# The third mixer of a two-layer hybrid block: one score product for both directions, one modulation job behind each step, fewer splits at stage borders, and transposes moved one stage ahead

## The chip, the core and the metric
One core of a Trainium2 chip runs one program. TensorE (PE) multiplies, VectorE (DVE) and ScalarE (ACT) work on elements, GpSimd (POOL) does little here, and SyncE (SP) issues the DMA transfers. Each has its own queue of instructions, run in order, and they are tied together by semaphores. The metric is device time in microseconds (us), the median of several runs.

## The reference
A diffusion backbone of two layers over 256 context and 256 latent tokens (512 columns in all, `T`) of width 1024. Each layer has a token-mixing part of four parallel mixers of 256 columns (RWKV-7, differential attention, HGRN2, mLSTM), read from one input projection and joined by one output projection, and a gated MLP with a centred convolution. Shift, scale and gate of each sub-layer come from a conditioning vector (`_adaln`: a matrix-vector product with `ada_w`). The third mixer, HGRN2, is a gated linear attention, run forward and on reversed time, and the two outputs are added:
```python
diff = b[:, :, :, None, :] - b[:, :, None, :, :]
pair_decay = jnp.where(causal[:, :, None], jnp.exp(jnp.minimum(diff, 0.0)), 0.0)
att = jnp.einsum('bhtd,bhsd,bhtsd->bhts', qc, kc, pair_decay)
o = jnp.einsum('bhtd,bhdv->bhtv', qc * jnp.exp(b), S) + jnp.einsum('bhts,bhsv->bhtv', att, vc)
```
Here `b` is the running sum of log forget gates, so the decay between two tokens is the exponential of a difference, per channel. The two directions have the same queries and values, and keys and gates of their own. Layer 1 needs outputs for the latent tokens only.

## The kernel before, in words
Tokens lie along the free axis, channels on the 128 partitions; 512 tokens are 4 blocks of 128. Activations are kept in SBUF from beginning to end and weights are streamed. All large products are made in three passes of a high and a low part (`product`, L235 to L237); the two parts of a weight tile are made by ACT (`split_high`, L224) and DVE (`split_low`, L228).

A layer is a row of stages, each a block of five instruction queues that ends when all five are done: `front` (modulation, first tiles of the input projection), `diff_attention`, `mlstm`, `hgrn`, `rwkv`, then the output projection and MLP. The input projection (`Projection`) runs through the first three: its tiles are shared out over the steps of those mixers. Tile t+2 is split while tile t is copied out of PSUM (`leave_act`, `leave_dve`; `act_turn`, `dve_turn` per step), so at each border the stage that ends has split one tile more than its successor needs to begin (`end + 1`).

In `hgrn` (L1510 on) the decays inside a block of 128 are factored by levels. At level l (0 to 6) the block is cut into pairs of halves of 2^l tokens; tokens of the one half attend to tokens of the other with respect to the value of `b` at the border, so that query and key factors are exponentials that stay at most 1. There are 7 levels and 2 directions d, so 14 steps `steps`, walked by all engines:
- DVE subtracts the border value (`exponents`, L1788); ACT takes exponentials for keys and queries (`exps`, L1922, L1925); DVE multiplies by queries (L1796) and keys (L1797) (`factors`);
- PE makes the scores into PSUM (L1669), 32 matmuls for two pairs of blocks in layer 0, 16 for one pair in layer 1;
- DVE takes the entries of that level out with a masked copy (`collect`, L1815) into `at`, 2 x 2048 columns, one matrix per direction, which POOL has zeroed (L1760).

Beside the steps run key decays (a subtraction on DVE, L1850, and an exponential of 1024 columns on ACT, L1955), keys, queries, transposes (L1652), products and states for what passes between blocks. The read-out multiplies `at` of both directions by the values (L1711).

Behind the scores also stand the **jobs**: the modulation products of parts of `ada_w` for what comes later. A job is four transfers of 512 KB into four slots (SP, L1612), each freed by the matmuls of the job before (PE, `job_blocks`, L446), a copy of the sums by ACT (`row_out`, L1934), a spread over the partitions by PE (L1637 for coefficients, L1639 for gates, once for each side, context and latent), and an addition by DVE (L465 or L1779). `HIDDEN` lists 10 jobs for layer 0 and 4 for layer 1, and `places(n)` shares them over the steps. The tail of `hgrn` prepares the low-rank parts and the keys of `rwkv` (table load L1972, scans L1447) and the norm. `rwkv` begins with 32 transposes on PE (L2093: V, be, ks, al), which ACT and DVE (L2456) copy out.

## Time and profile before
| what | value |
|---|---|
| median of 3 runs | 1746.48 us (1746.31 to 1747.27) |
| profiled execution | 1743.03 us |
| its span | 1740.9 us |
| mean granted TensorE clock | 0.956 |
| PE busy | 1595.0 us, 92% |
| DVE busy | 1089.4 us, 63% |
| ACT busy | 636.7 us, 37% |
| POOL busy | 75.5 us, 4% |

The span is the time between the first and the last instruction that the profile shows. Busy shares are a mean over stages that differ: most of PE's time lies in the projections and the MLP.

### The profile page before, as it was taken

Reading aid. Unit: us, or ns where it says so; the run is one execution under the profiler, and the core shown is the slowest. Engines: PE = TensorE matmul, PEld = TensorE weight load, DVE = VectorE, ACT = ScalarE, POOL = GpSimd, SP = SyncE. Lnnn points to the kernel's source line nnn. Section 1 sums busy time; section 2 is a strip of 40 time slices with the busy share of each in tenths; the row PEclk is TensorE's granted clock in tenths of the full one; section 3 lists DMA queues with packets and bytes.
Section 4 is the critical chain, followed back from the end, with each engine's and each line's share of the span. In section 5 each row is a group of like instructions: output and inputs, shape, how many; then the busy total and the mean of one; then the engine's idle time right before and its main releaser. Section 6 shows DMA issues by size and latency. Waiting matters only on the chain. (4 is left out here: it accounts for less than half of the span.)

```text
span 1740.9 us, 29515 instructions
## 1 busy us (share of the span) xinstructions
PE 1595.0 (92%) x12140; PEld 1267.4 (73%) x12140; DVE 1089.4 (63%) x1870; ACT 636.7 (37%) x1060; POOL 75.5 (4%) x112
## 2 busy tenths in 40 slices
PE   6999999878889999999999979999977799899997
PEld 4766776655678778888888867677764587678885
DVE  2287347887786674554453364745678867578776
ACT  4255222333531245222222252433243431366662
POOL 0000011200101000000000000000020100000000
PEclk8999999978999999999999989999978899999998
DMA  9411111077301034222223022112225101255551
GB/s 391 149 49 50 49 61 52 22 250 247 136 3 51 26 146 154 104 96 92 102 84 119 1 87 86 61 49 85 74 86 178 68 3 51 77 212 197 186 203 47
DMA packets 41622, 182.02 MB, mean 105 GB/s; under 512 B 4753, under 2 KB 5521, under 8 KB 33681
## 3 DMA queue, kind: packets, MB, share of 16 engines
q1 hardware_dynamic: 41488, 180.14, 29.0%
q8 instruction: 96, 1.57, 0.4%
q14 instruction: 38, 0.30, 0.1%
HBM read 179.08 MB, written 1.05 MB: 103 GB/s over the span
## 5 line engine op out<-in xcount | busy, mean ns | idle before, releaser
L235 PE MATMUL ps<-hr_in,wr_in 128*128 128x512 f32 (+1 forms) x544 | 221.8, 408 | 14.4 <-DVE wr_in L228 13.9
L236 PE MATMUL ps<-hr_in,wr_in 128*128 128x512 f32 (+1 forms) x544 | 209.1, 384 | 0.0
L237 PE MATMUL ps<-hr_in,wr_in 128*128 128x512 f32 (+1 forms) x544 | 208.5, 383 | 0.0
L235 PEld LDWEIGHTS ps<-hr_in,wr_in 128*128 128x128 f32 x544 | 108.4, 199 | 63.9 <-issue 35.4
L228 DVE TENSOR_TENSOR wr_in<-mix,wr_in 128x1024 fp32r<-128x1024 f32 x68 | 83.8, 1234 | 93.5 <-ACT wr_in L224 89.6
L235 PE MATMUL ps<-mix_r,work_r 128*128 128x512 f32 (+1 forms) x352 | 133.8, 380 | 1.6 <-DVE work_r L228 1.6
L236 PE MATMUL ps<-work_r 128*128 128x512 f32 (+1 forms) x356 | 135.1, 379 | 0.0
L228 DVE TENSOR_TENSOR work_r<-pr,work_r 128x2048 fp32r<-128x2048 f32 x38 | 86.9, 2288 | 67.7 <-ACT work_r L224 63.6
L237 PE MATMUL ps<-mix_r,work_r 128*128 128x512 f32 x320 | 124.5, 389 | 0.0
L237 PEld LDWEIGHTS ps<-hr_in,wr_in 128*128 128x128 f32 x544 | 108.3, 199 | 19.6
L236 PEld LDWEIGHTS ps<-hr_in,wr_in 128*128 128x128 f32 x544 | 108.8, 200 | 15.5 <-issue 0.2
L2988 PE MATMUL ps<-mix_r,work_r 128*128 128x512 f32 x336 | 116.7, 391 | 1.0 <-DVE mix_r L228 1.0
L224 ACT CAST wr_in<-mix 128x1024 fp32r<-128x1024 f32 x68 | 71.3, 1050 | 106.6 <-PE ps L237 102.5
L224 ACT CAST work_r<-pr 128x2048 fp32r<-128x2048 f32 x40 | 76.1, 1902 | 65.9 <-PE ps L237 65.9
L3293 ACT ACTIVATE pr<-work 128x512 f32<-128x512 f32 (+1 forms) x44 | 23.1, 525 | 192.9 <-DVE work L3161 192.9
L235 PE MATMUL ps<-work_r,mix_r 128*128 128x512 f32 x232 | 90.4, 390 | 1.0 <-DVE work_r L228 1.0
L236 PE MATMUL ps<-work_r,mix_r 128*128 128x512 f32 x232 | 90.3, 389 | 0.0
L2989 PE MATMUL ps<-mix_r,work_r 128*128 128x256 f32 x320 | 89.6, 280 | 0.0
L235 PEld LDWEIGHTS ps<-mix_r,work_r 128*128 128x128 f32 x352 | 66.2, 188 | 14.5 <-DVE work_r L228 2.0
L236 PEld LDWEIGHTS ps<-work_r 128*128 128x128 f32 x356 | 66.9, 188 | 12.5
L228 DVE TENSOR_TENSOR work_r<-ring,work_r 128x2048 fp32r<-128x2048 f32 x24 | 54.9, 2288 | 32.9 <-ACT work_r L224 30.4
L2988 PEld LDWEIGHTS ps<-mix_r,work_r 128*128 128x128 f32 x336 | 62.8, 187 | 15.5 <-issue 1.8
(525 smaller groups left out, 3312.1 us busy)
## 6 DMA issues: line engine op xcount, KB each, us to landing
mix<-in_w_in SPq DMA_DIRECT2D x68, 512.0 KB, 3.7
pr<-in_w_up SPq DMA_DIRECT2D x28, 1024.0 KB, 4.9
pr<-in_ada_w SPq DMA_DIRECT2D x40, 512.0 KB, 6.3
ring<-in_w_up SPq DMA_DIRECT2D x16, 1024.0 KB, 4.8
ring<-in_ada_w SPq DMA_DIRECT2D x28, 512.0 KB, 4.5
pr<-in_w_down SPq DMA_DIRECT2D x14, 1024.0 KB, 5.0
pr<-in_ada_w SPq DMA_DIRECT2D x8, 1024.0 KB, 15.6
work<-in_w_out SPq DMA_DIRECT2D x16, 512.0 KB, 4.1
```

What stands on the lines that cost most here:

```text
L224: return nc.scalar.copy(high, raw)
L228: return nc.vector.tensor_tensor(low, raw, high.bitcast(F32), ALU.subtract)
L235: nc.tensor.matmul(out, sh, mh, start=first, stop=False)
L236: nc.tensor.matmul(out, sh, ml, start=False, stop=False)
L237: return nc.tensor.matmul(out, sl, mh, start=False, stop=last)
L2988: nc.tensor.matmul(up_bank(f, v)[:, :], sh, hr[0][:, k * T:(k + 1) * T], start=k == 0, stop=False)
L2989: mm = nc.tensor.matmul(up_bank(f, v)[:, SIDE:], sl, hr[0][:, k * T + SIDE:(k + 1) * T], start=False, stop=k == KD - 1)
L3293: nc.scalar.activation(pr[:, f * T + lo0:(f + 1) * T], tb[:, (f % 2) * T + lo0:(f % 2 + 1) * T], ACT.Gelu_apprx_tanh).then_inc(S("gelu"), 1)
```

## The change
It has four parts.
- **Third mixer.** The steps are eight: the diagonal (`None`: raw queries times the sum of both directions' keys, taken out by a product with the identity, which also writes the zeros) and the seven levels in the order 0 to 4, 6, 5. A level's keys of both directions lie in one tile (the halves that are sooner in time for forward, later for backward) and so do its queries, and one score product serves both. `at` is one matrix of 2048 columns, so the read-out has half the matmuls. The last level (6, step `WHOLE`) is copied by ACT, 8 plain copies, rather than collected by DVE. The key decays are 16 exponentials of 128 columns on ACT with a bias each, without DVE's subtraction. The masks in the constants serve both directions.
- **Jobs.** One job stands directly behind each step's scores in layer 0 (8 jobs) and behind six of the eight in layer 1; jobs (1,2) and (1,3) replace (1,6) and (1,7) in the late list, which go into layer 1's third mixer. The gate's bias is loaded once and not for each side.
- **Borders.** The stage that ends no longer splits tile `end + 1`; the next stage does it at its beginning.
- **Transposes.** Those of V and ks (16) move from the beginning of `rwkv` to the end of `hgrn` on PE.

PE in the loop of layer 0, from the values' transposes on: scores of a step (L1669, then L1679), job matmuls (L446, then L447), coefficient spread (L1637, L1643), gate spread (L1639, L1645). Before:

```order
L1652 MATMUL ps<-const,pr 128x128 x8
L1669 MATMUL ps<-ring,work 128x128 x32
L446 MATMUL ps<-ring,cond 32x256 x8
L446 MATMUL ps<-pr,cond 32x256 x8
L1669 MATMUL ps<-ring,work 128x128 x16
L1637 MATMUL ps<-const,rowb 128x2 x4
L446 MATMUL ps<-ring,cond 32x256 x8
L446 MATMUL ps<-pr,cond 32x256 x8
L1669 MATMUL ps<-ring,work 128x128 x16
L1652 MATMUL ps<-const,pr 128x128 x8
```

and now:

```order
L1658 MATMUL ps<-const,pr 128x128 x8
L1679 MATMUL ps<-pr,work 128x128 x16
L447 MATMUL ps<-ring,cond 32x256 x8
L447 MATMUL ps<-pr,cond 32x256 x8
L1679 MATMUL ps<-ring,work 128x128 x16
L1643 MATMUL ps<-const,rowb 128x2 x4
L447 MATMUL ps<-ring,cond 32x256 x8
L447 MATMUL ps<-pr,cond 32x256 x8
L1645 MATMUL ps<-rowb,const 128x512
L1679 MATMUL ps<-ring,work 128x128 x16
L1645 MATMUL ps<-rowb,const 128x512
```

A job now stands behind each group of scores from the first on, and a level's two groups are one, made of the shared tiles.

DVE at the same place, from the first exponents (L1788, then L1797 and L1799). Before, up to the second collect:

```order
L1788 TENSOR_TENSOR work<-hx 128x1024 x2
L1796 TENSOR_TENSOR ring<-work,pr 128x1024
L1797 TENSOR_TENSOR work<-work,pr 128x1024
L1788 TENSOR_TENSOR work<-hx 128x1024
L1850 TENSOR_TENSOR pr<-hx 128x1024
L1796 TENSOR_TENSOR ring<-work,pr 128x1024
L1797 TENSOR_TENSOR work<-work,pr 128x1024
L1788 TENSOR_TENSOR work<-hx 128x1024
L1815 COPY_PREDICATED work<-const,ps 128x4x128 x4
L1850 TENSOR_TENSOR pr<-hx 128x1024
L1796 TENSOR_TENSOR ring<-work,pr 128x256x2
L1797 TENSOR_TENSOR work<-work,pr 128x256x2
```

and now, with the key sum (L1806), level 0's key copies (L1810), the factors (L1814, L1815), the diagonal (L1832) and masked collects (L1834):

```order
L1806 TENSOR_TENSOR work<-pr 128x1024
L1797 TENSOR_TENSOR work<-hx 128x512 x2
L1799 TENSOR_TENSOR work<-hx 128x1024 x2
L1810 COPY work<-pr 128x512 x2
L1815 TENSOR_TENSOR ring<-ring,pr 128x1024
L1799 TENSOR_TENSOR work<-hx 128x1024 x2
L1832 TENSOR_TENSOR work<-ps,const 128x4x128 x4
L1814 TENSOR_TENSOR work<-work,pr 128x256x2 x2
L1815 TENSOR_TENSOR ring<-ring,pr 128x1024
L1799 TENSOR_TENSOR work<-hx 128x1024 x2
L466 SCALAR_TENSOR_TENSOR modc<-ps,modb 128x8
L1834 COPY_PREDICATED work<-const,ps 128x4x128 x4
```

The key decays' subtraction (L1850) is gone, and two subtractions of 1024 columns now stand for one level where before each stood in a step of its own.

PE at the end of `hgrn` and the start of `rwkv` (L2093, then L1768 and L2128), before:

```order
L446 MATMUL ps<-pr,cond 32x256 x8
L946 MATMUL ps<-work,const 128x512
L446 MATMUL ps<-pr,cond 32x256 x8
L1568 UNCONDITIONAL_BRANCH
L2113 UNCONDITIONAL_BRANCH
L2093 MATMUL ps<-const,pr 128x128 x8
L2093 MATMUL ps<-const,ring 128x128 x24
L2137 MATMUL ps<-ring 128x128 x48
```

and now:

```order
L447 MATMUL ps<-pr,cond 32x256 x8
L1768 MATMUL ps<-const,pr 128x128 x8
L1768 MATMUL ps<-const,ring 128x128 x8
L1570 UNCONDITIONAL_BRANCH
L2148 UNCONDITIONAL_BRANCH
L2128 MATMUL ps<-const,ring 128x128 x16
L2170 MATMUL ps<-ring 128x128 x48
```

Of the 32 transposes 16 stand ahead of the stage's end (the branch) and 16 behind it.

The core of the diff:

```diff
-LAST = (((1, 6), (1, 7)), ((1, 8), (1, 9)))
-HIDDEN = (((0, 8), (0, 4), (0, 9), (0, 5), (1, 0), (0, 10), (1, 1), (0, 11), (1, 2), (1, 3)),
-          ((1, 4), (1, 5), (1, 10), (1, 11)))
+LAST = (((1, 2), (1, 3)), ((1, 8), (1, 9)))
+HIDDEN = (((0, 8), (0, 4), (0, 9), (0, 5), (1, 0), (0, 10), (1, 1), (0, 11)),
+          ((1, 6), (1, 7), (1, 4), (1, 5), (1, 10), (1, 11)))
+HIDDEN_AT = (range(8), (0, 1, 2, 4, 5, 6))
...
         for t in self.started(i):
             if t > self.first:
                 self.leave_act(act, t - 1)
-                self.high(act, t + 1)
+            self.high(act, t + 1)
...
             for t in range(proj.end):
-                proj.low(dve, t + 2)
+                if t + 2 <= proj.end:
+                    proj.low(dve, t + 2)
...
-            proj.high(act, proj.end + 1)
...
-    steps = [(d, l) for l in range(LEVELS) for d in range(2)]
+    steps = (None, *range(LEVELS - 2), LEVELS - 1, LEVELS - 2)
+    WHOLE = 6
...
+    def parts_at(n):
+
+        if n not in HIDDEN_AT[layer]:
+            return (), ()
+        q = HIDDEN_AT[layer].index(n)
+        return range(begins[q - 1] + 1 if q else 0, begins[q]), range(begins[q], begins[q] + 1)
+
+    late = range(begins[-1] + 1, PLACES)
...
+            for n in range(len(steps)):
+                ahead, behind = parts_at(n)
+                for p in ahead:
+                    job(p)
                 pe.wait_ge(S("kf"), n + 1)
+                moving = queries[n % 2] if n else tiles(pr, T_HQ, 2)
...
+                            mm = nc.tensor.matmul(score_bank(n, m, q)[:, b * P:(b + 1) * P], keys[n % 2][q * HD:(q + 1) * HD, t0:t0 + P],
+                                                  moving[q * HD:(q + 1) * HD, t0:t0 + P], start=True, stop=True)
...
+                for p in behind:
+                    job(p)
...
-        @block.gpsimd
-        def _(pool):
-            nc.gpsimd.memset(at[:, :], 0.0).then_inc(S("at0"), 1)
+            pe.wait_ge(S("kk_max"), 1)
+            pe.wait_ge(S("lora_out"), 8)
+            for src, bank in ((tiles(pr, T_V, 2), 0), (R.ks, 2)):
+                for j in range(TILES):
+                    for i in range(2):
+                        nc.tensor.transpose(ps[bank + j // 2][:, (j % 2) * 256 + i * P:(j % 2) * 256 + (i + 1) * P],
+                                            src[:, i * T + j * P:i * T + (j + 1) * P], ident)
...
             def exponents(n):
 
-                d, l = steps[n]
-                cv, dv = blocks(tiles(cum, 2 * d, 2), l), blocks(expo[d], l)
-                ref = (1 << l) - 1 if d == 0 else 1 << l
-                if n >= 2:
-                    dve.wait_ge(S("kf"), n - 1)
-                nc.vector.tensor_tensor(dv, cv, cv[:, :, :, ref:ref + 1].to_broadcast(list(cv.shape)),
-                                        ALU.subtract).then_inc(S("dv"), 1)
+                l = steps[n]
+                for d in range(2):
+                    cv, dv = blocks(tiles(cum, 2 * d, 2), l), blocks(tiles(expo[n % 2], 2 * d, 2), l)
+                    ref = (1 << l) - 1 if d == 0 else 1 << l
+                    if l == 0:
+                        ins = nc.vector.tensor_tensor(dv[:, :, :, 1 - d:2 - d], cv[:, :, :, 1 - d:2 - d], cv[:, :, :, d:d + 1], ALU.subtract)
+                    else:
+                        ins = nc.vector.tensor_tensor(dv, cv, cv[:, :, :, ref:ref + 1].to_broadcast(list(cv.shape)), ALU.subtract)
+                ins.then_inc(S("dv"), 1)
...
             def factors(n):
-                d, l = steps[n]
-                dve.wait_ge(S("exps"), n + 1)
-                if n >= 2:
-                    dve.wait_ge(S("s_mm"), len(pairs) * (n - 1))
-                nc.vector.tensor_tensor(later(queries[d], d, l), later(expo[d], d, l), later(tiles(pr, T_HQ, 2), d, l), ALU.mult)
-                nc.vector.tensor_tensor(sooner(keys[d], d, l), sooner(keys[d], d, l), sooner(tiles(pr, T_HF + 2 * d, 2), d, l),
-                                        ALU.mult).then_inc(S("kf"), 1)
+
+                l, k = steps[n], keys[n % 2]
+                if n == 0:
+                    nc.vector.tensor_tensor(two(k, layer), two(keys_of(0), layer), two(keys_of(1), layer), ALU.add).then_inc(S("kf"), 1)
+                    return
+                if l == 0:
+                    for d in range(2):
+                        nc.vector.tensor_copy(half(k, l, d == 1), half(keys_of(d), l, d == 1))
+                dve.wait_ge(S("exps"), n)
+                if l:
+                    for d in range(2):
+                        nc.vector.tensor_tensor(half(k, l, d == 1), half(k, l, d == 1), half(keys_of(d), l, d == 1), ALU.mult)
+                nc.vector.tensor_tensor(two(queries[n % 2], layer), two(queries[n % 2], layer), two(tiles(pr, T_HQ, 2), layer), ALU.mult)\
+                    .then_inc(S("kf"), 1)
...
             def collect(n):
-                d, l = steps[n]
-                B = 2 << l
+
+                l, done = steps[n], n - (n > WHOLE)
+                if n == WHOLE + 1:
+                    dve.wait_ge(S("at_whole"), 2 * len(pairs))
                 for m, jj in enumerate(pairs):
                     dve.wait_ge(S("s_mm"), len(pairs) * n + m + 1)
-                    o = d * 2048 + jj[0] * 512
                     for q in range(2):
-                        dst = at[:, o:o + 1024].rearrange("p (b q t) -> p b q t", b=4, q=2)[:, :, q, :]
+                        if n:
+                            dve.wait_ge(S("at"), 2 * len(pairs) * (done - 1) + 2 * m + q + 1)
+                        dst = at[:, jj[0] * 512:jj[0] * 512 + 1024].rearrange("p (b q t) -> p b q t", b=4, q=2)[:, :, q, :]
                         src = score_bank(n, m, q)[:, :].rearrange("p (b t) -> p b t", b=4)
-                        if l == 0:
-                            mask = c(C_BASE + d * P).bitcast(I32).rearrange("p (b t) -> p b t", b=1).to_broadcast([P, 4, P])
+                        mask = ident if n == 0 else c(C_BASE if l == 0 else C_LEVEL + l * P)
+                        if n == 0:
+                            ins = nc.vector.tensor_tensor(dst, src, mask.rearrange("p (b t) -> p b t", b=1).to_broadcast([P, 4, P]), ALU.mult)
                         else:
-                            part = slice(B // 2, B) if d == 0 else slice(0, B // 2)
-                            dst, src = (v.rearrange("p b (k t) -> p b k t", t=B)[:, :, :, part] for v in (dst, src))
-                            mask = halves(c(C_LEVEL + (d * LEVELS + l) * P).bitcast(I32), B, d == 0).to_broadcast(list(dst.shape))
-                        nc.vector.copy_predicated(dst, mask, src).then_inc(S("at"), 1)
+                            ins = nc.vector.copy_predicated(dst, mask.bitcast(I32).rearrange("p (b t) -> p b t", b=1).to_broadcast([P, 4, P]), src)
+                        ins.then_inc(S("at"), 1)
...
+            factors(0)
             exponents(1)
-            for n in range(len(steps)):
+            exponents(2)
+            for n in range(1, len(steps)):
+                ahead, behind = parts_at(n)
                 factors(n)
                 if n + 2 < len(steps):
                     exponents(n + 2)
-                if n == 1:
-                    dve.wait_ge(S("at0"), 1)
-                if n >= 1:
+                for p in ahead or behind:
+                    spread_out(p)
+                if n - 1 != WHOLE:
...
+            def collect_whole():
+
+                act.wait_ge(S("at"), 2 * len(pairs) * WHOLE)
+                for m, jj in enumerate(pairs):
+                    act.wait_ge(S("s_mm"), len(pairs) * WHOLE + m + 1)
+                    for q in range(2):
+                        for d in range(2):
+                            rows_, part = (slice(0, P // 2), slice(P // 2, P)) if d == 0 else (slice(P // 2, P), slice(0, P // 2))
+                            dst = at[rows_, jj[0] * 512:jj[0] * 512 + 1024].rearrange("p (b q t) -> p b q t", b=4, q=2)[:, :, q, part]
+                            ins = nc.scalar.copy(dst, score_bank(WHOLE, m, q)[rows_, :].rearrange("p (b t) -> p b t", b=4)[:, :, part])
+                        ins.then_inc(S("at_whole"), 1)
...
                 if n in KEYS_EXP_AT:
                     r = KEYS_EXP_AT.index(n)
-                    act.wait_ge(S("rest"), r + 1)
-                    nc.scalar.activation(tiles(kd, 2 * r, 2), tiles(kd, 2 * r, 2), ACT.Exp).then_inc(S("kd_exp"), 1)
+                    for b in range(2 * TILES):
+                        cv = tiles(cum, 2 * r, 2)[:, b * P:(b + 1) * P]
+                        ins = nc.scalar.activation(tiles(kd, 2 * r, 2)[:, b * P:(b + 1) * P], cv, ACT.Exp, bias=cv[:, end(r):end(r) + 1], scale=-1.0)
+                    ins.then_inc(S("kd_exp"), 1)
...
-            turns(tiles(pr, T_V, 2), (0, 1)).then_inc(S("vT"), 1)
             turns(be, (6, 7)).then_inc(S("beT"), 1)
-            turns(ks, (2, 3)).then_inc(S("kT"), 1)
...
-            t[:, a:a + P] = (s // (2 << l) == q // (2 << l)) & (s // (1 << l) != q // (1 << l)) & before
+            t[:, a:a + P] = (s // (2 << l) == q // (2 << l)) & (s // (1 << l) != q // (1 << l))
```

## Rows read from the trace of the kernel before
**Rows 1.** Windows: loop and tail of layer 0's third mixer, of layer 1's, and three microseconds
```profile
core 0: us, PE busy (x) PEld busy (x) DVE busy (x) ACT busy (x) POOL busy (x), PEclk, DMA share, GB/s
347.35:438.24 90.89, 74.97 (x874) 51.37 (x875) 76.26 (x131) 32.98 (x53) 3.51 (x1) 0.84 0.71 251
438.24:464.20 25.96, 21.40 (x215) 12.63 (x213) 20.14 (x32) 14.72 (x20) 0.00 (x0) 1.00 0.26 99
1295.80:1349.20 53.40, 40.72 (x451) 27.16 (x452) 45.47 (x96) 22.67 (x48) 3.52 (x1) 0.82 0.57 204
1349.20:1368.60 19.40, 14.74 (x118) 7.25 (x117) 17.48 (x29) 13.06 (x19) 0.00 (x0) 0.91 0.10 40
...
360.00:363.00 3.00, 2.48 (x23) 2.52 (x24) 3.00 (x5) 0.00 (x0) 0.00 (x0) 0.50 0.03 5
```

**Rows 2.** Groups by line, layer 0's third mixer: operation, tiles, count, busy us, mean ns, idle
```profile
L1788 DVE TENSOR_TENSOR work<-hx 128x1024 f32<-128x1024 f32 x14 | 17.1, 1224 | 0.7 <-PEq L1054 0.3
L1797 DVE TENSOR_TENSOR work<-work,pr 128x512 f32<-128x512 f32 x12 | 8.2, 681 | 0.0
L1815 DVE COPY_PREDICATED work<-const,ps 128x256 f32<-128x256 int32 x48 | 19.5, 489 | 5.9 <-PE ps L1669 5.7
L1815 DVE COPY_PREDICATED work<-const,ps 128x512 f32<-128x512 int32 x8 | 5.2, 721 | 0.0
L1779 DVE TENSOR_TENSOR gate<-gate,ps 128x512 f32<-128x512 f32 x8 | 5.5, 682 | 3.4 <-PE ps L1639 3.4
```

**Rows 3.** The same view of the third mixer of layer 1
```profile
L1788 DVE TENSOR_TENSOR work<-cum 128x512 f32<-128x512 f32 x14 | 9.6, 691 | 0.7 <-PEq L1054 0.3
L1797 DVE TENSOR_TENSOR work<-work,pr 128x256 f32<-128x256 f32 x12 | 5.0, 416 | 0.0
L1815 DVE COPY_PREDICATED work<-const,ps 128x256 f32<-128x256 int32 x24 | 10.2, 485 | 4.8 <-PE ps L1669 4.8
```

**Rows 4.** Timeline of PE, layer 0, one step: start, us, engine, line, operation, tiles
```profile
380.05 2.06 PE L1669 MATMUL ps<-ring,work 64*128 64x128 f32 x32
382.03 1.12 PE L1639 MATMUL ps<-rowb,const 128*128 128x512 f32 x2
383.09 1.07 PE L446 MATMUL ps<-ring,cond 128*32 128x256 f32 x16
```

**Rows 5.** Timeline of PE, layer 0, at the lower clock and at a wait for a transfer
```profile
360.52 3.79 PE L1669 MATMUL ps<-ring,work 64*128 64x128 f32 x32 [3.79 <-DVE work L1815]
364.23 1.93 PE L446 MATMUL ps<-ring,cond 128*32 128x256 f32 x16
...
417.75 2.30 PE L446 MATMUL ps<-ring,cond 128*32 128x256 f32 x16 [0.55 <-DMA ring<-in_ada_w]
423.63 2.72 PE L1669 MATMUL ps<-ring,work 64*128 64x128 f32 x22
```

**Rows 6.** Timeline of DVE at the end of layer 0's loop and the tail's first scan
```profile
435.12 3.12 DVE L1815 COPY_PREDICATED work<-const,ps 128x256 f32<-128x256 int32 x8
...
441.22 2.34 DVE L1447 TENSOR_TENSOR_SCAN hx<-work 128x512 f32<-128x512 f32 x2
```

**Rows 7.** Timelines at the start of layer 0's first mixer, PE and DVE
```profile
465.14 4.45 PE L2093 MATMUL ps<-const,ring 128*128 128x128 f32 x24
...
469.63 1.29 DVE L2456 COPY work<-ps 128x512 f32<-128x512 f32 x2 [4.17 <-PE ps L2093]
```

**Rows 8.** Timelines at two stage borders of layer 0: DVE and PE, then ACT and PE, then DVE
```profile
76.80 1.23 DVE L228 TENSOR_TENSOR wr_in<-mix,wr_in 128x1024 fp32r<-128x1024 f32 x1 [5.48 <-ACT wr_in L224]
...
78.42 2.43 PE L759 MATMUL ps<-pr,const 128*128 128x256 f32 x8 [2.01 <-PEq L481]
...
164.45 0.58 ACT L377 COPY pr<-ps 128x512 f32<-128x512 f32 x1 [1.67 <-PE ps L237]
...
167.56 0.43 PE L1076 MATMUL ps<-const,pr 64*128 64x64 f32 x4 [3.15 <-PEq L738]
...
174.56 0.19 DVE L1215 TENSOR_TENSOR pr<-pr 128x32 f32<-128x32 f32 x1 [1.35 <-ACT pr L1364]
```

115 lines of the change are left out of this document (49 added, 66 removed).

## Prediction
> **What bounds the kernel now.** Over the whole span TensorE is the busiest engine, but the change touches stretches where it is not what ends last, so I read the third mixer's stages first. The windows [rows 1] show four stretches. In layer 0 the loop over the score steps lasts 90.89 us, of which VectorE (DVE) works 76.26 and PE 74.97; the tail lasts 25.96, with DVE 20.14. In layer 1 the loop lasts 53.40 with DVE at 45.47 and PE at 40.72. The reader is to see that DVE is the fullest engine in each, that it leaves 14.6 us (90.89 - 76.26) and 7.9 us (53.40 - 45.47) idle in the two loops, and that ScalarE (ACT), 32.98 of 90.89, has room.
>
> The groups by line then say what DVE does in the loop [rows 2, 3] and the timelines what PE does in a step [rows 4, 5]. In a step at 2.4 GHz, the 32 score matmuls take 2.06 us, two gate spreads 1.12 and one half of a job's matmuls 1.07. From 360 to 363 the granted clock is 0.50, which is 1.2 GHz [rows 1], and there, after 3.79 us of idling for DVE, the same scores take 3.79 and the half job 1.93 [rows 5]. The mean granted clock of the loops is 0.84 and 0.82 [rows 1], so PE is at the lower level for a good part of them. The DMA wait also shows: from 417.75 to 423.63, 5.9 us, a job sits on PE waiting for its quarters [rows 5].
>
> At the two other places the waits are at stage borders. The first mixer of layer 0 begins with transposes whose last 24 take 4.45 us, and DVE waits 4.17 us for them [rows 7]. Between front and attention PE idles 2.01 us and between attention and the fourth mixer 3.15 us, each until the preceding stage's last engine is done [rows 8].
>
> **The third mixer, layer 0.** I count DVE's work, since DVE fills the loop. What goes: 14 exponent subtractions (17.1 us); 24 factor products of 512 columns at 0.681 and 4 of 1024 at about 1.22, together 21.2; the collects, 19.5 + 5.2 = 24.7; two subtractions of 1024 columns for the key decays, which ACT now does as a bias, 2.4 [rows 2]. That is 65.4 us. What comes: one key sum at 1.2; exponents of two directions on seven levels, of which level 0 works on half the columns: 2 x 0.68 + 12 x 1.224 = 16.1; factors: seven query products of 1024 columns, two copies of 512 and 12 key products of 512: 7 x 1.22 + 2 x 0.68 + 12 x 0.681 = 18.1; collects: the diagonal in four products at 0.682 (the row of the gate sum, which also reads PSUM) and six levels x 4 of 512 columns at 0.721: 20.0 [rows 2]. That is 55.4. DVE's work falls by 10.0 us. The collects gain little although there are half as many, because each now covers all 512 columns: 28 of them cost 20.0 where 56 cost 24.7.
>
> Of the 14.6 us that DVE was idle, I expect about 10 to go. Before, a step of one direction had two factor products, one subtraction and four collects, about 4.7 us of DVE, while PE had scores, spread and a job's part, so PE was often late. Now a step has about 8 us of DVE work (55.4 + the 10.9 of other DVE operations that stay, 66 us over 8 steps), against 2.06 of scores, 1.12 of spread and 2 x 1.07 of job, 5.3 us, for PE [rows 4]. DVE collects a step after the scores were issued, so PE has a whole step to deliver. The half-width products per level also halve PE's scores, from 14 x 2.06 = 29 to 8 x 2.06 = 16 us. The loop then falls by 10 + 10 = 20.
>
> The tail gives back some of it. Before, after the last collect at 435.12 to 438.24, the first scan starts at 441.22, 3.0 us later [rows 6]: the table load and low-rank products that precede it ran beside the last collects. With the loop shorter, and a job placed behind the very last scores, the last job's sums come before them. I put 3 us on that, the length of the present gap again. The halved read-out matmuls lie beside DVE and are worth nothing. Layer 0: **-17**. The ends are -22 (all idle but a few us gone, no give-back beyond 3) and -7 (idle time stays whole, 3 given back: -10 + 3).
>
> **The work moved to ACT.** The key decays become 16 small exponentials in place of two of 1024 columns, and one level's scores are copied by ACT, 8 copies. If each of the 24 took as long as the gate sum of 512 columns, 0.68, this would be 16 us more; even so ACT's 33 would be 49 of some 70 [rows 1, 2], and nothing waits for it except DVE's last collect, which comes a step later. I cost it at nothing; the cover is that slack of 20 us.
>
> **Third mixer, layer 1.** The same account at half width: gone are 9.6 of exponents, 12.8 of factors, 12.9 of collects and 2.4 of decays, 37.7; new are 0.7 + 9.1 + 10.7 + 10.0 = 30.5, by 0.691 and 0.416 for products and subtractions of 512 and 256 columns and 0.72 a collect [rows 2, 3]. DVE falls by 7.2. But this stage now has six jobs instead of four, and a quarter of a job is loaded only when its slot is free. By the wait of 5.9 us [rows 5], six jobs in a row cannot be over before about 6 x 5.9 = 35 us after the first transfer lands, some 9 us into the stage (5.9 for its landing behind scores of 1.9 and transposes), 44 in all, to which the last scores and collects (about 1.1 + 2 x 0.72) are added: 46.5 against 53.4. DVE's own floor is 45.5 - 7.2 = 38.3. I take **-6**, between +3 (the series case below) and -11 (the floor and half of the 7.9 us idle).
>
> **Start of the first mixer.** Before DVE's copy stand 32 transposes, and 16 of them leave. The first 8 run from the border at 464.2 [rows 1] to 465.14, 0.9 us, and go; of the next 24, which take 4.45, 8 go, 1.5 us [rows 7]. DVE's wait of 4.17 falls by 2.4 at most; I take 2.0. The moved transposes run on PE while DVE finishes the third mixer, so they cost nothing in layer 0, where PE waits at the end of the stage; in layer 1, where the last job's matmuls end nearer to the border, I take off 0.5. Sum 2 x 2.0 - 0.5: **-3.5**, between -4.3 and 0 (if the border waits for them).
>
> **Borders.** Splitting one tile less at the end of front, attention and fourth mixer takes a DVE subtraction of 1.23 us and an ACT cast off the last chain. Front to attention: of 2.01 us idle, about 0.6 (the final copy out of PSUM) has to stay, -1.4. Attention to fourth mixer: the copy ends at 165.03; with the 0.4 us that a border needs, PE would start at 165.4 instead of 167.56, -2.1 [rows 8]. The split is not gone, it is done at the next stage's beginning, and there the forget-gate row of the fourth mixer stands behind it: cast 1.05 and subtraction 1.23, less the 1.35 that DVE waited there already, gives back 0.9. So -1.4 and -1.2 in each of two layers: **-5**, between -1 and -7 (no give-back).
>
> **The sum**: -17 - 6 - 3.5 - 5 = -31.5 us. The profiled execution took 1743.03 us, 3.45 less than the median of 1746.48, so the changed kernel should show 1711.5 in such an execution and 1715 as a median. A difference of 0.2%, 3.5 us, is about what a measurement of this kernel can tell from none.
>
> **Rivals.**
> *PE and transfers in series, clock high.* If a step's scores, spread and the landing of a job follow one another, a step is 2.06 + 1.6 (the 1.12 of two spreads and half as much for the hand-over) + 5.9 = 9.6 us, and eight give 76.5, with 5.4 for the start and the last collect (2.3 + 3.1) 82 against 90.9: -9. In layer 1, with half the scores (1.1) and one spread (1.1), 6 x 8.1 and 8 for the two steps without a job and the ends are 57: +3. With 8.5 from borders and starts the total is -14: **1732**. For it speaks that one job now stands behind every step's scores, so a late quarter holds the next scores; against it that DVE's 8 us covers the transfer.
> *The slower side: the clock stays low.* The place is PE between two steps. DVE takes 8 us a step and PE has 5.3 of work, so PE idles more than before, and after idling 3.79 us it was found at granted clock 0.50 [rows 1, 5]. At 1.2 GHz, in series with the transfer, a step is 3.8 + 2.9 (the 1.6 at that level) + 5.9 = 12.6 us; eight, with the 5.4 grown to 9.8, are 110.6, +20; in layer 1 6 x (1.9 + 1.4 + 5.9) + 12.8 = 68, +15; less 8.5, +26: **1772**. It decides when a PE step exceeds DVE's 8 us. The Trainium skill (TensorE: Matmul & The Clock Gate, HAM oscillation) has this as a rule against the change: matmul bursts that alternate with waits are throttled again in each wait. The low means in rows 1 agree that it happens here; but the scores at 2.06 us [rows 4] show that steps with waits of a few us also run at the higher level.
> *The borders give nothing*, because the split delays the next stage as much as it freed the last: **1720**.
>
> **How the numbers follow.** Forecast 0.66, series 0.16, borders 0.13, low clock 0.05. The first three are all faster; of the series case I keep 0.03 for a result within 0.2%, so faster 0.92, same 0.03, slower 0.05. The range is 1702 (the far ends of all terms: -22 - 11 - 4 - 7 = -44) to 1732 (the series case); the low-clock case and the worst ends lie outside.
>
> **What would show it.** Right: layer 0's loop at about 71 us with DVE over 90% busy and a granted clock of 0.8 or more; layer 1's at about 47; the DVE wait at the start of the first mixer near 2; PE idle at the two borders near 0.6 and 1. Wrong: DVE idle in the loops as long as before, waiting for scores behind jobs that wait for transfers; long stretches at 0.50; a new wait at the fourth mixer's forget row longer than 2.3.

## The result and the profile after

The changed kernel takes 1731.05 us (1729.7 to 1735.37, four runs) against 1746.88 for the kernel before: ratio 0.991, 95% interval 0.9889 to 0.9931. A second comparison gave 1728.33 against 1746.29, again 0.991 (0.9877 to 0.9942). It is faster, by 15.8 and 18.0 us, about half of the 31.5 forecast. The profiled execution took 1729.70 us with a span of 1727.9, 13.0 less than before.

The stages, from the first instruction behind one border to the first behind the next in the timelines of the two profiled executions, in us:

| stage | layer 0: before, after | difference (forecast) | layer 1: before, after | difference (forecast) |
|---|---|---|---|---|
| front | 78.4, 77.1 | -1.3 (-1.4) | 45.7, 44.3 | -1.4 (-1.4) |
| attention | 89.2, 86.2 | -3.0 (-2.1) | 71.3, 67.7 | -3.6 (-2.1) |
| fourth mixer | 179.9, 186.8 | +6.9 (+0.9) | 149.0, 152.5 | +3.5 (+0.9) |
| third mixer | 116.8, 102.2 | -14.6 (-17) | 72.8, 75.9 | +3.1 (-6) |
| first mixer | 160.1, 157.2 | -2.9 (-2.0) | 150.3, 150.3 | 0 (-1.5) |
| projection and MLP | 405.5, 405.6 | +0.1 (0) | 222.0, 222.0 | 0 (0) |

The windows of the third mixer after, to be held against [rows 1] (loop and tail of layer 0, loop and tail of layer 1; length, then busy time of PE, its loads, DVE, ACT and POOL, granted clock, DMA share, GB/s):

```profile
350.10:416.29 66.19, 52.71 (x628) 37.11 (x628) 61.98 (x93) 31.35 (x67) 0.00 (x0) 0.90 0.73 271
416.29:452.37 36.08, 28.26 (x173) 13.52 (x173) 21.19 (x32) 17.70 (x25) 0.00 (x0) 0.76 0.15 60
1279.66:1334.36 54.70, 43.47 (x430) 26.07 (x430) 37.07 (x74) 25.71 (x66) 0.00 (x0) 0.76 0.82 290
1334.36:1355.60 21.24, 16.91 (x123) 8.70 (x123) 18.10 (x32) 13.09 (x20) 0.00 (x0) 0.92 0.01 2
```

In layer 0 the loop is 24.7 us shorter (90.89 to 66.19) and DVE fills it, 61.98 us. The tail is 10.1 us longer (25.96 to 36.08). In layer 1 DVE's work fell to 37.07, as forecast (38.3), and yet the loop is 1.3 us longer: 17.6 us of it DVE is idle.

The groups of DVE, layer 0, which answer to [rows 2] (count, busy us, mean ns, idle before and its releaser), and two of layer 1:

```profile
L1834 DVE COPY_PREDICATED work<-const,ps 128x512 f32<-128x512 int32 x24 | 15.4, 719 | 0.0
L1799 DVE TENSOR_TENSOR work<-hx 128x1024 f32<-128x1024 f32 x12 | 14.1, 1217 | 0.0
L1815 DVE TENSOR_TENSOR ring<-ring,pr 128x1024 f32<-128x1024 f32 x7 | 8.5, 1216 | 0.0
L1788 DVE TENSOR_TENSOR gate<-gate,ps 128x512 f32<-128x512 f32 x8 | 5.5, 682 | 12.6 <-PE ps L1645 12.5
```

```profile
L1834 DVE COPY_PREDICATED work<-const,ps 128x512 f32<-128x512 int32 x12 | 8.1, 726 | 9.4 <-issue 5.8 <-PE ps L1679 3.6
L466 DVE SCALAR_TENSOR_TENSOR modc<-ps,modb 128x8 f32<-128x8 f32 x2 | 0.3, 163 | 4.8 <-PE ps L1643 4.8
```

The collects, exponents and products cost per piece what was forecast. The idle time stands at the gate sums in layer 0 (12.6 us, nearly all one wait, which lies in the tail) and, in layer 1, at collects and coefficient sums. For 5.8 us of the collects' wait the view names no releaser; it is the wait for the last scores, shown below.

The tail's wait in layer 0, answering to [rows 6], on DVE, then PE, then ACT:

```profile
413.72 2.57 DVE L1834 COPY_PREDICATED work<-const,ps 128x512 f32<-128x512 int32 x4
428.82 0.69 DVE L1788 TENSOR_TENSOR gate<-gate,ps 128x512 f32<-128x512 f32 x1 [12.53 <-PE ps L1645]
430.22 2.34 DVE L1446 TENSOR_TENSOR_SCAN hx<-work 128x512 f32<-128x512 f32 x2
...
418.23 1.08 PE L447 MATMUL ps<-pr,cond 128*32 128x256 f32 x8 [0.61 <-DMA pr<-in_ada_w]
423.00 3.78 PE L1709 MATMUL ps<-pr,par 64*128 64x512 f32 x4 [3.69 <-ACT pr L2009]
426.71 2.07 PE L1645 MATMUL ps<-rowb,const 128*128 128x512 f32 x2
...
419.98 1.28 ACT L2007 ACT_TABLE_LOAD   x1
```

The last job's last quarter lands late, its matmuls run to 419.3; only then ACT copies its row and, behind it, loads the table for the low-rank activations. PE waits 3.69 us for these and then runs at its lower level: the spread behind the low-rank matmuls takes 2.07 us, where [rows 4] had 1.12. DVE waits 12.53 us for that spread before it may begin its scans, 13.9 us after the last collect's end (3.0 before).

In layer 1's loop (PE, then DVE) scores stand behind jobs that wait for quarters:

```profile
1286.82 0.64 PE L447 MATMUL ps<-pr,cond 128*32 128x256 f32 x8 [1.15 <-DMA pr<-in_ada_w]
1288.20 0.86 PE L447 MATMUL ps<-pr,cond 128*32 128x256 f32 x8 [0.74 <-DMA pr<-in_ada_w]
1288.99 2.08 PE L1679 MATMUL ps<-ring,work 64*128 64x128 f32 x16
...
1329.84 1.08 PE L447 MATMUL ps<-pr,cond 128*32 128x256 f32 x8 [0.65 <-DMA pr<-in_ada_w]
1330.85 2.08 PE L1679 MATMUL ps<-ring,work 64*128 64x128 f32 x16
...
1292.90 0.17 DVE L466 SCALAR_TENSOR_TENSOR modc<-ps,modb 128x8 f32<-128x8 f32 x1 [4.80 <-PE ps L1643]
1333.03 1.33 DVE L1834 COPY_PREDICATED work<-const,ps 128x512 f32<-128x512 int32 x2 [5.81 <-issue]
```

The scores at 1288.99 have had their factors since 1283.2 (by DVE's timeline), but the first job and its waits for transfers stand ahead of them on PE; DVE waits 4.80 us for the spread behind those scores. The last collect, at 1333.03, begins 0.1 us after the end of the last scores, which stand behind the sixth job. The first job's matmuls end at 1289.06 and the sixth's at 1330.92, so a job comes every 8.4 us on average. The transfers do not run without a pause either, though their share of that loop is 0.82. From 1279 to 1340 the view of waits gives for SP (time, times, longest)

```profile
SPq L1619 <- PE ps L447: 33.1, 17, 7.4
```

that is 33.1 us of waiting for slots that job matmuls had still to free, 5.5 us a job. For the four jobs before, the same view gives 22.3 us, which is as much a job.

### The profile page after: what moved, and what is told of

Read it like the earlier page. It is cut to its first block and busy times, and to the rows that moved or that the text cites. A ratio compares the mean times of both kernels' runs of the same rounds, so it can differ in the third digit from the quotient of the medians.

```text
span 1727.9 us, 28779 instructions
## 1 busy us (share of the span) xinstructions
PE 1583.7 (92%) x11804; PEld 1251.0 (72%) x11804; DVE 1068.9 (62%) x1812; ACT 640.4 (37%) x1096; POOL 70.0 (4%) x110
## 5 line engine op out<-in xcount | busy, mean ns | idle before, releaser
L236 PEld LDWEIGHTS ps<-hr_in,wr_in 128*128 128x128 f32 x544 | 110.0, 202 | 63.1 <-issue 36.4
L229 DVE TENSOR_TENSOR work_r<-pr,work_r 128x2048 fp32r<-128x2048 f32 x38 | 87.0, 2288 | 68.0 <-ACT work_r L225 63.9
L238 PEld LDWEIGHTS ps<-hr_in,wr_in 128*128 128x128 f32 x544 | 109.5, 201 | 19.8
L237 PEld LDWEIGHTS ps<-hr_in,wr_in 128*128 128x128 f32 x544 | 109.8, 202 | 15.8 <-issue 0.2
L225 ACT CAST wr_in<-mix 128x1024 fp32r<-128x1024 f32 x68 | 71.3, 1050 | 103.5 <-PE ps L238 103.5
L225 ACT CAST work_r<-pr 128x2048 fp32r<-128x2048 f32 x40 | 76.0, 1901 | 66.8 <-PE ps L238 66.2
L236 PEld LDWEIGHTS ps<-mix_r,work_r 128*128 128x128 f32 x352 | 66.2, 188 | 14.6 <-DVE work_r L229 2.1
L237 PEld LDWEIGHTS ps<-work_r 128*128 128x128 f32 x356 | 66.9, 188 | 12.5
## 6 DMA issues: line engine op xcount, KB each, us to landing
pr<-in_ada_w SPq DMA_DIRECT2D x8, 1024.0 KB, 16.1
```

Source lines behind the costliest of these rows:

```text
L225: return nc.scalar.copy(high, raw)
L229: return nc.vector.tensor_tensor(low, raw, high.bitcast(F32), ALU.subtract)
L236: nc.tensor.matmul(out, sh, mh, start=first, stop=False)
L237: nc.tensor.matmul(out, sh, ml, start=False, stop=False)
L238: return nc.tensor.matmul(out, sl, mh, start=False, stop=last)
```

## The experiments

All were compared with the kernel before on the same chip. That kernel's median was 1746.88 us beside the changed kernel, 1745.63 beside borders, tail and four jobs, 1746.29 beside changed again, first six, gate row and old transposes, and 1742.49 beside the last four, so kernels of different groups are held together by the ratio. The table gives the median, the ratio to before with its 95% interval, and from each profile the length of four stages. In brackets stands what the clock took: the sum over windows of one microsecond of one minus the granted clock. Each length is that of one execution.

| kernel | median | ratio (interval) | fourth mixer, layer 0 | third, 0 | fourth, 1 | third, 1 |
|---|---|---|---|---|---|---|
| before | 1746.88 | | 179.9 (7.1) | 116.8 (14.7) | 149.0 (8.9) | 72.8 (11.5) |
| changed | 1731.05 | 0.9910 (0.9889-0.9931) | 186.8 (15.4) | 102.2 (15.2) | 152.5 (12.4) | 75.9 (14.6) |
| changed, again | 1728.33 | 0.9910 (0.9877-0.9942) | 182.3 (9.1) | 100.9 (12.9) | 151.5 (8.7) | 76.2 (14.9) |
| borders alone | 1740.42 | 0.9973 (0.9953-0.9993) | 180.7 (5.5) | 117.4 (14.6) | 154.2 (14.2) | 72.6 (11.3) |
| old borders | 1735.13 | 0.9940 (0.9915-0.9966) | 179.8 (7.1) | 103.9 (18.1) | 152.0 (13.8) | 78.1 (18.1) |
| tail | 1719.30 | 0.9846 (0.9797-0.9895) | 182.4 (9.2) | 96.1 (11.1) | 154.1 (14.3) | 70.4 (7.8) |
| four jobs | 1715.58 | 0.9825 (0.9787-0.9863) | 180.7 (5.5) | 104.4 (18.1) | 152.5 (12.4) | 62.3 (7.8) |
| first six | 1728.90 | 0.9915 (0.9890-0.9940) | 186.8 (15.3) | 102.1 (13.5) | 152.4 (12.4) | 78.6 (14.7) |
| gate row | 1723.22 | 0.9878 (0.9845-0.9911) | 181.8 (10.8) | 103.2 (16.1) | 147.0 (6.9) | 76.3 (13.1) |
| old transposes | 1729.30 | 0.9908 (0.9877-0.9940) | 185.6 (12.5) | 103.3 (14.5) | 150.3 (6.8) | 73.9 (10.2) |
| busy | 1787.90 | 1.0259 (1.0234-1.0284) | 180.7 (7.3) | 138.2 (7.7) | 154.2 (14.2) | 100.7 (4.4) |
| tail + gate row | 1714.11 | 0.9841 (0.9812-0.9869) | 178.7 (5.4) | 96.3 (11.3) | 148.5 (10.7) | 71.4 (9.5) |
| 10 + 4 jobs | 1727.05 | 0.9922 (0.9893-0.9950) | 182.4 (7.3) | 115.1 (19.8) | 152.5 (12.4) | 64.5 (9.5) |
| all | 1715.29 | 0.9841 (0.9811-0.9871) | 181.8 (10.8) | 107.8 (14.4) | 149.0 (10.4) | 63.9 (9.6) |

**Borders.** The kernel before with the diff's border hunks alone, and the changed kernel without them. One of the eight hunks:
```diff
-            proj.high(act, proj.end + 1)
```

> The kernel before with only the later splits at the stage borders. Of the changed kernel the profile says: front 1.3 us shorter in each layer, attention 3.0 and 3.6 shorter, but the fourth mixer 6.9 (layer 0) and 3.5 (layer 1) longer, with more of its time at the lower granted clock. Theory A: the longer fourth mixer comes from the border change (the split at its beginning, and a start at another moment, which changes where the clock falls), not from the third mixer. Then the fourth mixer of layer 0 takes about 186.7 us here as well, against 179.8 before, and the total is 1746 to 1749, no gain. Rival B: the borders are worth what was predicted, -5, and the fourth mixer is longer by chance or because of other parts: then it takes 179 to 181 us and the total is 1738 to 1742.

> The changed kernel with the borders as before (the ending stage splits one tile more again). Theory A: the fourth mixer of layer 0 is back at 179.8 us, front and attention take 4.2 us more, so the total is the changed kernel's within 3 us, 1728 to 1733. Rival B: the gain of front and attention is lost and nothing comes back, 1738 to 1741.

Theory A fell: with the same instructions the fourth mixer of layer 0 took 180.7 us, not 186.7. The borders alone are worth -0.27% (interval -0.07 to -0.47%), 4.7 us, and taking them out of the changed kernel leaves 0.994 of before. The first total is rival B's; the second, 1735.13, lies between the two. Both fit the forecast of 5 us, with a wide interval.

**The changed kernel again.**

> The changed kernel itself, once more, beside the kernel before on the same chip. In three experiments whose fourth mixer of layer 0 has the same instructions as the changed kernel's, that stage took 180.7, 182.4 and 180.7 us and not 186.8. Theory G: how often the granted clock falls in the fourth mixer differs between executions of one program, so the 6.9 us that the changed kernel's profile shows there are mostly chance: this profile shows 180 to 184 us, while the third mixers stay at 102 and 76 within 2.5 us; the median is 1729 to 1734. Rival H: the changed kernel's own placing makes it, and the stage is at 186 to 188 us again.

Theory G held: 182.3, with a median just below the one that it named. In nine executions whose fourth mixer of layer 0 has the same instructions (all but before, old borders and the three with the gate row moved) it took 180.7 three times, 182.3 to 182.4 three times, 185.6 once and 186.8 twice. What the clock took goes along with it, from 5.5 to 15.4 us. So most of the 6.9 us of the stage table differs between executions. The mean of the nine is 183.2, against 179.9 and 179.8 in the only two executions with the old borders; whether some 3 us belong to the new borders is not settled.

**The tail.** Low-rank activations ahead of the last job's row on ACT; their first matmuls between the last scores and the last job on PE; the first gate addition behind the scans on DVE.
```diff
+                if n == len(steps) - 1:
+                    pe.wait_ge(S("low_rank"), 1)
+                    wait_collected(pe, idle_from)
+                    lora(0, 0)
                 for p in behind:
                     job(p)
```


> The changed kernel with the low-rank activations and their table load ahead of the last job's row, the first low-rank products between the last scores and the last job, and the last job's first gate addition behind the scans on VectorE. In the changed kernel the first scan of layer 0 starts 13.9 us after the last collect (3.0 before). Theory C: this wait is made by the job that stands behind the last scores, so that here the scans start within 4 us of the last collect, the third mixer of layer 0 takes 92 to 95 us instead of 102.3, layer 1's 74 to 76, and the total falls to 1720 to 1724. Rival D: TensorE at the lower clock bounds the tail in any case (busy 31 of its last 36 us): the scans start sooner but the stage ends at most 3 us sooner, total 1727 to 1730.

DVE's last coefficient sum, last collect and first scan, and PE's low-rank matmuls, in this kernel:

```profile
417.08 0.17 DVE L466 SCALAR_TENSOR_TENSOR modc<-ps,modb 128x8 f32<-128x8 f32 x1 [7.43 <-PE ps L1643]
417.19 2.56 DVE L1835 COPY_PREDICATED work<-const,ps 128x512 f32<-128x512 int32 x4
420.44 2.34 DVE L1446 TENSOR_TENSOR_SCAN hx<-work 128x512 f32<-128x512 f32 x2
...
412.37 2.88 PE L1668 MATMUL ps<-pr,par 64*128 64x512 f32 x4 [1.70 <-ACT pr L2009]
```

The scans start 0.7 us after the collect's end (419.75 to 420.44). The stage fell to 96.1, short of the 92 to 95 that theory C named: the last collect comes later in the stage, because a coefficient sum ahead of it now waits 7.43 us for a spread that stands behind the low-rank matmuls. The total, 1719.30, is slightly below C's; its interval still touches the changed kernel's. The stage is the firmer sign: it took 96.1 and 96.3 us in the two kernels with this edit alone or with the gate row, and 100.9 to 104.4 in the seven that have the changed kernel's loop of layer 0 without this edit. Layer 1 gained more than expected (70.4), but there the clock took 7.8 instead of 14.6, so the edit's own part is not known.

**Jobs in layer 1.**
```diff
-          ((1, 6), (1, 7), (1, 4), (1, 5), (1, 10), (1, 11)))
-HIDDEN_AT = (range(8), (0, 1, 2, 4, 5, 6))
+          ((1, 4), (1, 5), (1, 10), (1, 11)))
+HIDDEN_AT = (range(8), (2, 4, 5, 6))
```


> The changed kernel without the two jobs (1,6) and (1,7) in layer 1's third mixer: their transfers, matmuls, rows and spreads are left out and their 16 columns of coefficients set to zero, so shift and scale of layer 1's MLP are not computed; the other four jobs keep their steps 2, 4, 5, 6. Theory E: layer 1's third mixer did not get shorter (75.9 us, 72.9 before) because its steps wait on TensorE behind jobs that wait for their transfers: then it takes 65 to 68 us here and the total is 1720 to 1724. Rival F: the steps themselves (lower clock, hand-overs between the engines) hold it: it takes 72 us or more, total 1727 or more.

The whole third mixer of layer 1 here, and in the changed kernel, as windows:

```profile
1277.96:1340.27 62.31, 47.69 (x473) 28.63 (x473) 54.69 (x104) 37.58 (x83) 0.00 (x0) 0.87 0.52 188
```

```profile
1279.66:1355.60 75.94, 60.39 (x553) 34.77 (x553) 55.17 (x105) 38.80 (x86) 0.00 (x0) 0.81 0.59 210
```

DVE works as long (54.69 and 55.17), but 13.6 us are gone from the stage, more than theory E named, or 6.8 us a job. This includes the clock, which took 14.6 us in the one and 7.8 in the other. Where it took alike, in two kernels below that differ in the jobs (tail + gate row with six, 71.4 us, all with four, 63.9; the clock 9.5 and 9.6), two jobs cost 7.5 us. How much of a job's cost is the wait and how much the clock that falls in it is not separated. Then the same six jobs at other steps:
```diff
-HIDDEN_AT = (range(8), (0, 1, 2, 4, 5, 6))
+HIDDEN_AT = (range(8), range(6))
```

> The changed kernel with layer 1's six jobs behind steps 0 to 5 instead of 0, 1, 2, 4, 5, 6. In the changed kernel the transfers pause from about 1309 to 1317 us, at the step that has no job, since all four slots are full. Theory I: the transfers are what layer 1's loop waits for, so without the pause it ends 4 to 6 us sooner: third mixer of layer 1 70 to 72 us instead of 75.9, total 1725 to 1728. Rival J: TensorE's order alone matters and each job costs its 6.8 us wherever it stands (two jobs cost 13.6 us): 75 to 77 us, total 1730 to 1733.

No gain (78.6; this execution, 1739.70 us, is the slowest of eight, whose median is 1728.90). The wait only moved. One job waits 2.81 us for a quarter, and DVE 7.80 us for the spread behind it. The last two lines are windows (length, busy time of PE, its loads, DVE, ACT and POOL, granted clock, DMA share, GB/s):

```profile
1312.76 1.08 PE L447 MATMUL ps<-ring,cond 128*32 128x256 f32 x8 [2.81 <-DMA ring<-in_ada_w]
...
1322.72 0.69 DVE L1788 TENSOR_TENSOR gate<-gate,ps 128x512 f32<-128x512 f32 x1 [7.80 <-PE ps L1645]
...
1320.00:1322.00 2.00, 2.00 (x7) 1.11 (x5) 0.00 (x0) 0.12 (x1) 0.00 (x0) 0.50 0.16 64
1322.00:1324.00 2.00, 2.00 (x25) 0.80 (x28) 1.28 (x3) 0.00 (x0) 0.00 (x0) 0.77 0.00 0
```

The stage is nearer to rival J's 75 to 77 us, but the run does not decide: the transfers pause here as well, from 1320 to 1324 (shares of 0.16 and 0.00). In the changed kernel they did so from 1310 to 1314 (0.19 and 0.05), for half as long as the expectation said. So the pause was moved and not taken out.

**Ten and four jobs.** The distribution of before, (1,6) and (1,7) late in layer 0 again; two jobs behind steps 2 and 6.
```diff
+HIDDEN_AT = ((0, 1, 2, 2, 3, 4, 5, 6, 6, 7), (2, 4, 5, 6))
+        r = q + HIDDEN_AT[layer].count(n) - 1
+        return range(begins[q - 1] + 1 if q else 0, begins[q]), range(begins[q], begins[r] + 1)
```


> The changed kernel with the jobs of the kernel before: ten in layer 0's third mixer (two each behind steps 2 and 6, one behind the others), four in layer 1's (behind steps 2, 4, 5, 6), (1,6) and (1,7) late in layer 0 again. Nothing is left out. Theory R: what a job costs depends on whether VectorE's work covers its transfer: layer 1's third mixer falls to 62 to 64 us as when two jobs were left out, layer 0's grows by 2 to 6 from 101 to 104, and the total falls by 8 to 11, to 1717 to 1722. Rival S: a job costs 6 to 7 us wherever it stands: layer 0 grows by 12 to 14 and the total stays at 1727 to 1731.

Rival S: layer 1 fell by 11 to 12 us (64.5 against 75.9 and 76.2), layer 0 grew by 13 to 14 (115.1 against 102.2 and 100.9), the total stood still (0.9922 and 0.9910 of before). A job thus cost 6 to 7 us in either layer in these executions, the clock's part included. A step that DVE would fill ends up waiting for a spread behind a quarter (PE, then DVE, then the loop's window, read as above, and its group of gate sums):

```profile
379.30 1.08 PE L447 MATMUL ps<-pr,cond 128*32 128x256 f32 x8 [1.06 <-DMA pr<-in_ada_w]
380.62 1.08 PE L447 MATMUL ps<-pr,cond 128*32 128x256 f32 x8 [0.23 <-DMA pr<-in_ada_w]
...
384.52 0.69 DVE L1789 TENSOR_TENSOR gate<-gate,ps 128x512 f32<-128x512 f32 x1 [3.96 <-PE ps L1646]
...
346.60:434.62 88.02, 70.75 (x720) 42.11 (x720) 63.67 (x96) 33.26 (x71) 0.00 (x0) 0.79 0.75 265
...
L1789 DVE TENSOR_TENSOR gate<-gate,ps 128x512 f32<-128x512 f32 x8 | 5.5, 687 | 20.2 <-PE ps L1646 20.2
```

In this loop DVE works 63.67 of 88.02 us and idles 24.35, of which 20.2 stand at the gate sums; before, it idled 14.6.

With the jobs as before, the shared products leave layer 0's stage at 115.1 against 116.8 and layer 1's at 64.5 against 72.8. In this placing, most of layer 0's -14.6 is thus the two jobs that left it, and layer 1 paid for them. Whether another placing of the ten jobs would do better was not tried.

**Keeping PE busy.** Eight full matmuls ahead of each job.
```diff
+                    keep_busy(E, 8, 6)
```


> The changed kernel with 8 full matmuls of 128 x 512 (about 1.8 us at 2.4 GHz), whose result nobody reads, on TensorE ahead of every job in both third mixers, in the time in which it mostly waits for transfers. Theory P: the lower clock after these waits is what holds layer 1's loop (14.6 to 14.9 us are lost to it in that stage): the granted clock rises, and the stage takes 72 us or less instead of 76. Rival Q: the transfers set the pace, the scores are cheap at either level: the stage takes 75 us or more, even if less is lost to the clock, and the total is 1728 to 1736.

The dose was wrong. By the group of these matmuls in layer 0 they kept PE busy for 56.7 us, 7.1 a job, not 1.8:

```profile
L455 PE MATMUL ps<-const 128*128 128x512 f32 x128 | 56.7, 595 | 0.0
```

The 64 matmuls stand there as 128 records, two for each, so one of them takes 0.89 us. What the clock took fell to 7.7 and 4.4 us, but the added work hides what that was worth. The run settles nothing between P and Q, and the clock's part in layer 1's loop stays open.

**The forget-gate row.**
```diff
+            dve.wait_ge(S("lnf"), 1)
+            nc.vector.tensor_tensor(lf3, lb3, la3, ALU.subtract).then_inc(S("lf"), 1)
             for i in range(HEAD):
                 proj.dve_turn(dve, i)
-            dve.wait_ge(S("lnf"), 1)
-            nc.vector.tensor_tensor(lf3, lb3, la3, ALU.subtract).then_inc(S("lf"), 1)
```


> The changed kernel with the fourth mixer's forget-gate row ahead of the tile split on VectorE. Theory K: TensorE's wait of 2.4 us for that row (none before) goes, and the fourth mixers are 1 to 2.4 us shorter each, as far as the clock's chance lets it be seen; the row of the wait is gone in the trace, total 1727 to 1731. Rival L: the split is late for the second tile instead, the wait moves there and nothing is gained.

PE's group for this row around layer 0's border, in the changed kernel and here:

```profile
L1092 PE MATMUL ps<-const,pr 128*4 128x128 f32 x40 | 6.2, 323 | 2.4 <-DVE pr L1216 2.4
```

```profile
L1092 PE MATMUL ps<-const,pr 128*4 128x128 f32 x40 | 4.7, 272 | 0.3 <-DVE pr L1214 0.3
```

The wait is all but gone. By the view of waits of that stage, PE waits 0.5 us more for split tiles (2.0 for 1.5), so little of it moved: theory K, with a total below the one it named. The median is 5.1 us below the changed kernel's on that chip, more than two waits of 2.4 us can give, and the intervals overlap; but layer 1's fourth mixer took 147.0, 148.5 and 149.0 in the three kernels with this edit and 150.3 to 154.2 in the nine without it.

**The transposes.** V and ks back at the first mixer's beginning.
```diff
+            turns(tiles(pr, T_V, 2), (0, 1)).then_inc(S("vT"), 1)
             turns(be, (6, 7)).then_inc(S("beT"), 1)
+            turns(ks, (2, 3)).then_inc(S("kT"), 1)
```

> The changed kernel with the 16 transposes of V and ks back at the beginning of the first mixer. Theory M: VectorE's first copy comes 2.6 us later after the stage's start in both layers and the third mixers keep their length, so the total is 4 to 6 us more, 1734 to 1737. Rival N: the transposes stood on the path at the end of layer 1's third mixer, which gets 2 us shorter: 1732 to 1734.

DVE's first copy in the changed kernel (layer 0), answering to [rows 7], and here in layers 0 and 1:

```profile
455.15 1.29 DVE L2489 COPY work<-ps 128x512 f32<-128x512 f32 x2 [1.56 <-PE ps L2128]
```

```profile
458.31 1.29 DVE L2484 COPY work<-ps 128x512 f32<-128x512 f32 x2 [4.17 <-PE ps L2121]
...
1356.92 1.29 DVE L2484 COPY work<-ps 128x512 f32<-128x512 f32 x2 [2.50 <-PE ps L2121]
```

The wait falls from 4.17 to 1.56, 2.6 us, where the transposes ran at the lower clock; in this execution layer 1 ran them at the higher one and the old order waits only 2.50, 0.9 more. Layer 1's third mixer was 2.0 to 2.3 us shorter without them, but the clock took 4.4 to 4.7 less there. The totals, 1729.30 and 1728.33, don't tell the two kernels apart, and both M and N had named a higher one.

**Both repairs, and all.** Tail and gate row together, then with ten and four jobs as well.

> The changed kernel with both repairs: the low-rank part ahead of the last job, and the forget-gate row ahead of the split. If the two were measured rightly alone (-9 and -5 in the medians), they add up, since they lie in different stages: 1714 to 1719, faster than the changed kernel and than either repair. If one of the two was the clock's chance: 1719 to 1724.

> The changed kernel with both repairs and with ten jobs in layer 0 and four in layer 1. Theory R, with the repairs adding up: 1706 to 1712. Rival S: 1714 to 1720, no better than the two repairs alone.

With both repairs the median is 1714.11, ratio 0.9841 (0.9812 to 0.9869), an interval that lies below both of the changed kernel's. It beats both kernels. That the two add up is not shown: 1714.11 is in the range that was named for that, but the kernel before, too, was 3 to 4 us faster beside it, and the tail alone had 0.9846. The other distribution of jobs adds nothing (1715.29, 0.9841; third mixers 11.5 us longer in layer 0, 7.5 shorter in layer 1), rival S again.

## Why the prediction was half right

The direction, the bound by DVE in layer 0, and DVE's unit costs held. The sum was twice too large. By the stage table the two profiled executions fall short of the forecast by 18.5 us: 9.1 of it in layer 1's third mixer, 8.6 in the fourth mixers (of which up to 6 in layer 0 differs between executions of the same instructions), 2.4 in layer 0's third mixer; the rest cancels.

- **Layer 0's loop**, -20: it became -24.7, DVE's work falling by 14.3 (10.0 forecast) and its idle time by 10.4 (about 10 forecast) to 4.2 of 66.2 us. That the idle time came out is luck. The step that failed is "DVE collects a step after the scores were issued, so PE has a whole step to deliver": with ten jobs, DVE idles 24.35 us, more than before, and the whole stage gains 1.7 us. In the placing that was tried, it is thus the two jobs' leaving that emptied the loop of waits, and I costed that at nothing.
- **Layer 0's tail.** The step that failed is the size of the give-back, "I put 3 us on that, the length of the present gap again". It is 10.1 us. I had seen that the last job's sums come before the scans, but not followed the chain: row, table load, low-rank matmuls, spread, in that order on in-order queues, behind a quarter that lands at 418. The tail kernel shortens the stage by 6.
- **Layer 1's third mixer**, -6, is the largest miss: +3.1. The step that failed is "six jobs in a row cannot be over before about 6 x 5.9 = 35 us ... 46.5 against 53.4". It lets jobs follow one another while steps go on beside them, and its 5.9 us is misread: in these rows of the kernel before, which stand between the two lines of [rows 5],

```profile
421.38 1.08 PE L446 MATMUL ps<-pr,cond 128*32 128x256 f32 x8 [1.33 <-DMA pr<-in_ada_w]
422.62 1.08 PE L446 MATMUL ps<-pr,cond 128*32 128x256 f32 x8 [0.16 <-DMA pr<-in_ada_w]
```

only 1.5 us of it is waiting for quarters, and the rest is the job's own matmuls at the lower level. A job with its scores and spread took 8.4 us; the sixth was over 51.3 us into the stage, not 44. A slot is freed only by matmuls that stand behind scores. DVE's floor was right (37.07 for 38.3); the idle time beside it was 17.6. The rival of PE and transfers in series comes nearest here: it had 8.1 us a job. Its +3 was for the loop, which grew by 1.3; the rest of the stage's +3.1 is the tail, and its clock was to stay high, where the mean was 0.76. I gave it 0.16 for both layers at once, where it should have been weighed stage by stage.
- **Start of the first mixer**, -3.5: the wait fell by 2.6 in each layer, but layer 1's stage is no shorter (150.3 and 150.3); why stays open.
- **Borders**, -5: the border kernel shows 4.7 (1.2 to 8.2). Inside it two errors seem to cancel. Front and attention fell by 9.3 us in the two layers, 7.0 forecast; of the difference, attention's share goes with the clock, which took 1.7 us less there in each layer. PE's idle time fell to 0.52 and 0.93 us, as forecast, while the forget-gate row was dearer than 0.9: I set the 1.35 us that DVE idled against cast and split, but the cast starts only behind the logarithm on ACT. PE waits 2.40 us there, answering to [rows 8]:

```profile
77.16 1.97 PE L762 MATMUL ps<-pr,const 128*128 128x256 f32 x8 [0.52 <-PEq L482]
...
163.35 0.43 PE L1077 MATMUL ps<-const,pr 64*128 64x64 f32 x4 [0.93 <-PEq L741]
172.67 3.50 PE L1092 MATMUL ps<-const,pr 128*4 128x128 f32 x17 [2.40 <-DVE pr L1216]
...
171.29 1.23 DVE L229 TENSOR_TENSOR wr_in<-mix,wr_in 128x1024 fp32r<-128x1024 f32 x1 [2.28 <-ACT wr_in L225]
172.43 0.18 DVE L1216 TENSOR_TENSOR pr<-pr 128x32 f32<-128x32 f32 x1
```

A smaller misreading: since one matmul of this type stands as two records, the row of "two gate spreads" in [rows 4] is one, and a gate's job has two of 1.12 us.

The other rivals: the clock at its lower level throughout did not come; loops ran at 0.90 and 0.76 (0.84 and 0.82 before, [rows 1]). The rule from the Trainium skill that was weighed there (TensorE: Matmul & The Clock Gate, HAM oscillation) agrees with layer 0's tail, where PE's idle time grew from 4.6 to 7.8 us and the mean clock fell from 1.00 to 0.76. The sums of idle time do not show it in the loops: in layer 0's PE idled 18% before and 20% after, and the clock rose; in layer 1's it idled 24% and 21%, and the clock fell from 0.82 to 0.76. Which waits took it there is not shown. [Rows 4], which were held against the rule, show a step in which PE does not wait.

## What to carry to other kernels

Price a hidden job by the stage that it goes to: it costs nothing only if what it makes its in-order queue wait for is covered there. Here moving two jobs moved their price along and left the total as it was. When a loop gets shorter, follow by name the chain that used to end beside its last steps, since it becomes the tail. Read a long stretch on an engine line by line before calling it a wait. And look at stages of several executions before explaining a few microseconds of a PE-bound one.
